# Gated delta layer's seam: panel splits ahead of the barrier, the first convolution first on VectorE, projections between the small products

## The chip, the cores and the metric

One core of one Trainium2 chip runs the kernel. The metric is the device time of one execution in microseconds (us).

## The reference, cut to what matters

The program computes two pairs of layers on 512 tokens of width 1024, all in float32: first a block with two attention mixers, each followed by a SwiGLU feed-forward layer, then a gated delta layer (GDN) and a gated linear attention layer (GLA), each with a layer norm behind it. The change lies at the start of the gated delta layer:

```
p    = x @ w_in                                   # 8 heads: q, k (128 wide), v (256), gate (256); and b, a
qkv  = silu(causal_conv(p[qkv], conv_w))          # 4 taps, per channel
q, k = l2norm(q), l2norm(k)
beta = sigmoid(b);  g = -exp(a_log) * softplus(a + dt_bias)
gc   = cumsum(g) in chunks                        # decays exp(gc_i - gc_j)
o    = gated_delta_rule(q, k, v, g, beta)         # a triangular solve per chunk, a state carried on
y    = (rmsnorm(o) * norm_w * silu(gate)) @ w_out
x    = layer_norm(DEEP_ALPHA * x + y)
```

## The kernel before, in words

**Precision.** Each float32 operand of a large matmul is split into an upper part (a cast, `high`, or a copy on ScalarE) and a lower part (the rest, `low`, on VectorE). `mm3` then issues three matmuls for one: upper by upper, upper by lower, lower by upper (lines 223 to 225 of the profile). Weights come in panels of 128 x 2048 (1 MB) in a ring of four slots; `landed`, `used` and `split` are semaphores of a slot: loaded, released by TensorE, and split into `hi_ring` and `lo_ring`. Line 195 is the load, 216 and 219 are `high` and `low`.

**Two blocks.** The program has two blocks with a barrier of all engines between them (line 4095 in the profile). The first ends with the second feed-forward layer and the "early" part of the gated delta layer. There, SP loads the three panels of head 0 (slots 1, 2 and 3), the constants and `ba_w`, the small weight for beta and alpha. VectorE splits slot 1's panel, then alternates: a residual addition `dve_ffn_add` (line 1782), and for the piece before it the lower part, for which ScalarE's `act_gdn_early` (line 2546) has made the upper part. TensorE's `pe_gdn_early` does 7 of 8 steps of the first projection, `project(0, 0)`. The second block begins with `pe_gdn`, `act_gdn`, `dve_gdn` and `sp_gdn`; GpSimd adds the eight pieces of x at its start (`pool_total`, lines 3325 and 3328).

**The seam behind the barrier.** The queues' orders are written out by hand. TensorE: the last step of `project(0, 0)` (3 matmuls), `project(0, 1)` (24 matmuls of 512 columns), `beta_alpha` (16; lines 2585, 2586), half of `project(0, 2)` (12), `turn_beta_alpha` (line 2593), `q_sums` (line 244), `key_products` (line 2645), `cumulate` (lines 2599, 2601), `pe_ln_mean` (line 3296), the other half of `project(0, 2)`, `project(0, 3)` (24), `row_decays` (line 2651), and then `chain(0, None, 1)`. Projections share two banks of PSUM, so `project(h, 2)` waits for the convolution of 0 and `project(h, 3)` for that of 1.

VectorE: the split of `ba_w`, of panels 2 and 3, the taps (line 3027), `convolve(0, 0)` and `convolve(0, 1)` (one operation on line 3036 and three on 3038 each), the beta/alpha arithmetic (lines 3236 to 3246), the norms of q and k (3069 to 3077), the accumulated decays (3251, 3252), `convolve(0, 2)`, `columns_of` (3044 to 3052), `log_decays` (3063, 3064), its chain. ScalarE: the copy of the beta/alpha rows (line 2987), Silu of the first two convolutions (`convolved`, line 2873), the square of q, Exp and Ln for the decay (2992 to 2995), Ln of the norms, Exp and Sigmoid for the columns (2998, 2999), Silu of the third, the mean's copy, `decays` (2901 to 2904). Changing the function often costs an `ACT_TABLE_LOAD`.

**The chain** of a head solves the triangular system by doubling, six levels; each level is a pair of small products on TensorE (line 2756 and 2774) with VectorE's mask or addition between (3167, 3173). Ahead of it stand the decays and the first mask (A and Qh, lines 3146, 3150), which line 2744's turn of 64-column blocks waits for. Between the small products TensorE has "fills": in head 0 these are `project_gate(0, t)` for t = 0 to 3 (24 matmuls of 256 columns each), then the projections of head 1:

```
            def first_fill(part):
                ...
                elif p is None:
                    project_gate(i, 0, part * DC // 2, (part + 1) * DC // 2)
```

`first_fill(0)` stands before the turn, `first_fill(1)` behind it, then level 1's first product, `fill(1)`, its step product (line 2774) and `fill(2)`. VectorE answers the turn (line 3159), then does `convolve(0, 3)`, the taps of head 1 and two pieces of centring, and after that level 1's first product (line 3167), which the step product waits for. Heads 1 to 6 run in a loop, the last by itself; the change touches none of them.

Of the kernel before, what the change touches and what calls it, by code (L numbers as in the profile page):

```python
# [104 lines left out]
def build_in(nc, io, ctx):  # L105
# [2437 lines left out]
    def act_gdn_early(act):  # L2543
        for c in range(DC):
            act.wait_ge(S("ffn_added"), after("ffn1", "added", c + 1))
            nc.scalar.copy(h_hi[:, c, :], xT[:, c, :]).then_inc(S("g_x_upper"), 1)

    def dve_gdn_early(dve):
        for c in range(DC + 1):
            if c < DC:  # L2550
                dve_ffn_add(dve, "ffn1", c)
            if c:
                dve.wait_ge(S("g_x_upper"), c)
                low(h_lo[:, c - 1, :], xT[:, c - 1, :], h_hi[:, c - 1, :]).then_inc(S("ffn_x_split"), 1)

# [24 lines left out]
    def pe_gdn(pe):  # L2580
        def beta_alpha():

            pe.wait_ge(S("g_ba_split"), 1)
            for k in range(DC):
                mm(ps[0:BA_ROWS, 0, :], ba_parts[:, k, :], h_hi[:, k, :], start=k == 0, stop=False)
                last = mm(ps[0:BA_ROWS, 0, :], ba_parts[:, k, :], h_lo[:, k, :], start=False, stop=k == DC - 1)
            last.then_inc(S("g_ba_rows"), 1)
# [110 lines left out]
        def chain(i, p, h):  # L2698

            def first_fill(part):  # L2700
                if h is None:
                    output_part(p, *((0, 5), (5, 8))[part])
                elif p is None:
                    project_gate(i, 0, part * DC // 2, (part + 1) * DC // 2)
                else:
                    output(p, part, part + 1)

            def fill(place):
                if h is None:
                    start = 8 + 4 * (place - 1) - max(0, place - 8)  # L2710
                    output_part(p, start, start + (4 if place < 8 else 3))
                elif place < 4:
                    if p is None:
                        project_gate(i, place)
                    else:
                        output(p, 2 * place, 2 * place + 2)
                else:
                    c, half = divmod(place - 4, 2)
                    project(h, c, half * DC // 2, (half + 1) * DC // 2, gated=p is None)
# [125 lines left out]
        project(0, 1, 0, DC, first=True)  # L2845
        beta_alpha()
        project(0, 2, 0, DC // 2, first=True)
        turn_beta_alpha()
        q_sums(0)
# [3 lines left out]
        project(0, 2, DC // 2, DC, first=True)  # L2853
# [16 lines left out]
    def act_gdn(act):  # L2870
# [20 lines left out]
        def squares(h):  # L2891
            act.wait_ge(S("g_silu"), h * 4 + 2)
# [92 lines left out]

        act.wait_ge(S("g_ba_rows"), 1)
        nc.scalar.copy(ba_rows, ps[0:BA_ROWS, 0, :]).then_inc(S("g_ba_saved"), 1)
        convolved(0, 0)
        convolved(0, 1)
# [5 lines left out]
        nc.scalar.activation(z_l[:, :, :], z_e[:, :, :], ACT.Ln, bias=1.0).then_inc(S("g_zl"), 1)  # L2995
        norms(0)
        act.wait_ge(S("g_cum_cols"), 1)
        nc.scalar.activation(col_all(LAST), ps[:, 7, 0:TT * GH].rearrange("p (t h) -> p t h", t=TT), ACT.Exp).then_inc(S("g_col_exp"), 1)
        nc.scalar.activation(col_all(BETA), ba[:, :, 0:GH], ACT.Sigmoid).then_inc(S("g_col_exp"), 1)
# [9 lines left out]
    def dve_gdn(dve, link):  # L3009
# [215 lines left out]
        w, hi, lo = ba_w[:, :, :], ba_parts[:, :, 0:2 * GH], ba_parts[:, :, 2 * GH:BA_ROWS]  # L3225
        link(high(hi, w))
        low(lo, w, hi)
        nc.vector.tensor_tensor(ba_pairs, ident[0:BA_ROWS, 0:2 * GH], ident[0:BA_ROWS, 2 * GH:BA_ROWS], ALU.add).then_inc(S("g_ba_split"), 1)
        split_panel(dve, link, 2, 0)
        link(nc.vector.memset(U[second, :, first], 0.0))  # L3230
        conv_taps(0)
        split_panel(dve, link, 3, 0)
        convolve(0, 0)
        convolve(0, 1)
# [11 lines left out]
        nc.vector.tensor_copy(col_all(G), z_e[:, :, :])  # L3246
        q_variances(0)
# [787 lines left out]
    with nc.Block() as block:  # L4035
# [21 lines left out]
        def _(dve):  # L4057
# [16 lines left out]
            dve_gdn_early(dve)  # L4074
# [213 lines left out]
```

## Time and profile before

| | us |
|---|---|
| median of 3 runs | 2162.68 (2158.27 to 2166.95) |
| profiled execution, its span | 2162.8 |
| TensorE busy | 2092.5 |
| VectorE busy | 1475.1 |
| ScalarE busy | 958.6 |
| mean granted TensorE clock | 0.983 |

The page gives the span of the profiled execution and no other time for it; it is within 0.2 us of the median of the runs. Times in the trace count from the span's start. The barrier opens at 1280.86, and the first block takes the 1280 us before it. Only the some 60 us behind the barrier are at issue; where TensorE stands still there, and at which clock it runs, is to be read in the trace.

### The profile page before, as it was taken

The numbers are of one execution on the slowest core, as the hardware profiler recorded it, in microseconds if no ns is written. First come the engines' busy times: TensorE is split into PE (matmuls) and PEld (weight loads), VectorE is DVE, ScalarE is ACT, GpSimd is POOL, SyncE is SP. The second block draws the span as 40 slices with busy tenths as digits, with TensorE's granted clock in tenths as the row PEclk, the third lists the DMA queues.
The fourth block names the chain that finished last, engine by engine and source line by source line (L and its number), as shares of the span: only waits on it lengthen the run. The fifth ranks groups of instructions, "written<-read, shape, count | busy, mean of one in ns | idle before, by whom it ended". The sixth has DMA issues, their size and how long they took to land. (4 is left out here: it accounts for less than half of the span.)

```text
span 2162.8 us, 37677 instructions
## 1 busy us (share of the span) xinstructions
PE 2092.5 (97%) x15185; PEld 1802.0 (83%) x15185; DVE 1475.1 (68%) x2901; ACT 958.6 (44%) x1853; POOL 80.8 (4%) x47
## 2 busy tenths in 40 slices
PE   8998999999999999999999989999999999899997
PEld 8996667899988977889998867878887888688886
DVE  5347884988854677598886465666666666576566
ACT  5336872555400367345550014434443444356554
POOL 1110000000000300000000020000000000020000
PEclk9999999999999999999999998999999999999998
DMA  5230001232332320123323221111111110112211
GB/s 181 97 117 21 2 2 59 88 117 98 108 117 85 108 74 21 59 70 103 112 90 135 89 77 59 59 60 58 58 58 58 58 58 34 55 46 98 79 40 40
DMA packets 30666, 159.37 MB, mean 74 GB/s; under 512 B 3392, under 2 KB 3904, under 8 KB 17856
## 3 DMA queue, kind: packets, MB, share of 16 engines
q1 hardware_dynamic: 30240, 157.24, 20.5%
q8 instruction: 98, 1.61, 0.3%
q14 instruction: 40, 0.33, 0.0%
q10 hardware_dynamic: 288, 0.20, 0.0%
HBM read 155.33 MB, written 2.10 MB: 73 GB/s over the span
## 5 line engine op out<-in xcount | busy, mean ns | idle before, releaser
L224 PE MATMUL ps<-late_parts,panel_upper 128*128 128x256 f32 (+1 forms) x1376 | 460.2, 334 | 0.0
L223 PE MATMUL ps<-late_parts,panel_upper 128*128 128x256 f32 (+1 forms) x1260 | 433.6, 344 | 2.6 <-issue 1.8
L225 PE MATMUL ps<-late_parts,panel_parts 128*128 128x256 f32 (+1 forms) x1260 | 425.6, 338 | 0.0
L219 DVE TENSOR_TENSOR panel_parts<-panel_sb,panel_upper 128x512 fp32r<-128x512 f32 (+1 forms) x334 | 329.1, 1011 | 12.8 <-ACT panel_upper L723 8.4
L223 PE MATMUL ps<-panel_upper,hT_parts 128*128 128x256 f32 (+2 forms) x964 | 297.5, 309 | 7.3 <-DVE h_lower L911 7.3
L225 PE MATMUL ps<-panel_upper,h_lower 128*128 128x256 f32 (+2 forms) x964 | 285.4, 296 | 0.0
L224 PE MATMUL ps<-panel_parts,hT_parts 128*128 128x256 f32 (+2 forms) x964 | 284.3, 295 | 0.0
L224 PEld LDWEIGHTS ps<-late_parts,panel_upper 128*128 128x128 f32 x1376 | 260.2, 189 | 26.0 <-issue 0.2
L223 PEld LDWEIGHTS ps<-late_parts,panel_upper 128*128 128x128 f32 x1260 | 238.2, 189 | 32.9 <-issue 2.4
L225 PEld LDWEIGHTS ps<-late_parts,panel_parts 128*128 128x128 f32 x1260 | 239.2, 190 | 28.7
L223 PE MATMUL ps<-hT_parts,panel_upper 128*128 128x512 f32 (+1 forms) x508 | 203.8, 401 | 10.0 <-DVE arena_sb L3038 5.8
L223 PEld LDWEIGHTS ps<-panel_upper,hT_parts 128*128 128x128 f32 x964 | 184.5, 191 | 12.1 <-issue 7.9
L225 PE MATMUL ps<-hT_parts,panel_parts 128*128 128x512 f32 (+1 forms) x508 | 194.3, 382 | 0.0
L225 PEld LDWEIGHTS ps<-panel_upper,h_lower 128*128 128x128 f32 x964 | 185.0, 192 | 3.1
L224 PEld LDWEIGHTS ps<-panel_parts,hT_parts 128*128 128x128 f32 x964 | 184.0, 191 | 3.5
L224 PE MATMUL ps<-h_lower,panel_upper 128*128 128x512 f32 x432 | 174.4, 404 | 0.0
L1525 ACT CAST panel_upper<-panel_sb 128x512 fp32r<-128x512 f32 x230 | 132.6, 621 | 12.5 <-DVE panel_sb L1640 11.4
L223 PEld LDWEIGHTS ps<-hT_parts,panel_upper 128*128 128x128 f32 x508 | 96.7, 190 | 35.1 <-DVE arena_sb L3038 6.3
L225 PEld LDWEIGHTS ps<-hT_parts,panel_parts 128*128 128x128 f32 x508 | 96.8, 191 | 20.6
L224 PEld LDWEIGHTS ps<-h_lower,panel_upper 128*128 128x128 f32 x432 | 82.6, 191 | 17.6 <-issue 0.8
L2926 ACT COPY arena_sb<-ps 128x256 f32<-128x256 f32 (+1 forms) x40 | 14.9, 372 | 173.9 <-PE ps L2761 138.5
L3038 DVE SCALAR_TENSOR_TENSOR arena_sb<-ps,arena_sb 128x511 f32<-128x511 f32 (+2 forms) x96 | 71.9, 748 | 3.4
(531 smaller groups left out, 3787.6 us busy)
## 6 DMA issues: line engine op xcount, KB each, us to landing
panel_sb<-ffn_gate_up_w SPq DMA_DIRECT2D x76, 512.0 KB, 4.4
panel_sb<-gdn_w SPq DMA_DIRECT2D x24, 1024.0 KB, 4.8
panel_sb<-ffn_down_w SPq DMA_DIRECT2D x22, 1024.0 KB, 4.8
panel_sb<-nsa_w SPq DMA_DIRECT2D x13, 1024.0 KB, 5.0
panel_sb<-gla_w SPq DMA_DIRECT2D x12, 1024.0 KB, 4.8
panel_sb<-gdn_out_w SPq DMA_DIRECT2D x8, 1024.0 KB, 4.8
panel_sb<-ffn_gate_up_w SPq DMA_DIRECT2D x6, 1024.0 KB, 4.8
panel_sb<-nsa_out_w SPq DMA_DIRECT2D x4, 1024.0 KB, 4.7
```

The source lines that it names most:

```text
L219: return engine.tensor_tensor(out, src, hi.bitcast(F32), ALU.subtract)
L223: mm(out, w_hi, x_hi, start=start, stop=False, skip_group_check=skip_group_check)
L224: mm(out, w_hi, x_lo, start=False, stop=False, skip_group_check=skip_group_check)
L225: return mm(out, w_lo, x_hi, start=False, stop=stop, skip_group_check=skip_group_check)
L1525: nc.scalar.copy(hi, plain).then_inc(S("ffn_high"), 1)
L2926: nc.scalar.copy(Xh[r, :, :], ps[r, 3, 0:TT * HALF].rearrange("p (t c) -> p t c", t=TT)).then_inc(S("g_x"), 1)
L3038: last = nc.vector.scalar_tensor_tensor(conv[n][:, back:T], src[:, 0:T - back], hconv[:, n, 3 - back:4 - back], conv[n][:, back:T], ALU.mu ...
```

## The change

Ahead of the barrier: ScalarE makes the upper part of panel 2 before, and of panel 3 after its eight casts of x; VectorE makes the lower part of panel 2 before the residual additions, and the split of `ba_w` (with `ba_pairs`) behind them. Behind the barrier: VectorE begins with the taps and the first convolution, then the lower part of panel 3; the second convolution moves behind the beta/alpha arithmetic. ScalarE does Silu of the first convolution before the copy of the beta/alpha rows, the square of q before the second Silu, and the Sigmoid directly behind the Ln. TensorE does `beta_alpha` before `project(0, 1)`, `turn_beta_alpha` in its middle, and all of `project(0, 2)` before `q_sums`. In head 0's chain, `first_fill(0)` is all of `project_gate(0, 0)` and `first_fill(1)` the first half of `project_gate(0, 1)`, with the other half left to `fill(1)`.

```diff
     def act_gdn_early(act):
+        def upper(slot):
+            act.wait_ge(landed[slot], (act_panels.done[slot] + 1) * 16)
+            nc.scalar.copy(hi_ring[slot][:, :, :], ring[slot][:, :, :]).then_inc(S("g_early_upper"), 1)
+
+        upper(2)
         for c in range(DC):
...
+        upper(3)
+
+    def dve_gdn_early(dve, link):
+        dve.wait_ge(S("g_early_upper"), 1)
+        low(lo_ring[2][:, :, :], ring[2][:, :, :], hi_ring[2][:, :, :]).then_inc(split[2], 1)
         for c in range(DC + 1):
...
+        dve.wait_ge(S("gdn_const_landed"), 32)
+        w, hi, lo = ba_w[:, :, :], ba_parts[:, :, 0:2 * GH], ba_parts[:, :, 2 * GH:BA_ROWS]
+        link(high(hi, w))
+        low(lo, w, hi)
+        link(nc.vector.tensor_tensor(ba_pairs, ident[0:BA_ROWS, 0:2 * GH], ident[0:BA_ROWS, 2 * GH:BA_ROWS], ALU.add))
...
         def beta_alpha():
-            pe.wait_ge(S("g_ba_split"), 1)
...
                 elif p is None:
-                    project_gate(i, 0, part * DC // 2, (part + 1) * DC // 2)
+                    project_gate(i, *((0, 0, DC), (1, 0, DC // 2))[part])
...
                     if p is None:
-                        project_gate(i, place)
+                        project_gate(i, place, DC // 2 if place == 1 else 0, DC)
...
         project(0, 0, DC - 1, DC, first=True)
-        project(0, 1, 0, DC, first=True)
         beta_alpha()
-        project(0, 2, 0, DC // 2, first=True)
+        project(0, 1, 0, DC // 2, first=True)
         turn_beta_alpha()
+        project(0, 1, DC // 2, DC, first=True)
+        project(0, 2, 0, DC, first=True)
         q_sums(0)
         key_products(0, 3)
         cumulate()
         pe_ln_mean(pe, 0, GDN_MEAN_BANK)
-        project(0, 2, DC // 2, DC, first=True)
         project(0, 3, 0, DC, first=True)
...
         def squares(h):
-            act.wait_ge(S("g_silu"), h * 4 + 2)
+            act.wait_ge(S("g_silu"), h * 4 + 1)
...
+        convolved(0, 0)
         act.wait_ge(S("g_ba_rows"), 1)
         nc.scalar.copy(ba_rows, ps[0:BA_ROWS, 0, :]).then_inc(S("g_ba_saved"), 1)
-        convolved(0, 0)
-        convolved(0, 1)
         squares(0)
...
         nc.scalar.activation(z_l[:, :, :], z_e[:, :, :], ACT.Ln, bias=1.0).then_inc(S("g_zl"), 1)
+        nc.scalar.activation(col_all(BETA), ba[:, :, 0:GH], ACT.Sigmoid).then_inc(S("g_col_exp"), 1)
+        convolved(0, 1)
         norms(0)
         act.wait_ge(S("g_cum_cols"), 1)
         nc.scalar.activation(col_all(LAST), ...
-        nc.scalar.activation(col_all(BETA), ba[:, :, 0:GH], ACT.Sigmoid).then_inc(S("g_col_exp"), 1)
         convolved(0, 2)
...
-        w, hi, lo = ba_w[:, :, :], ba_parts[:, :, 0:2 * GH], ba_parts[:, :, 2 * GH:BA_ROWS]
-        link(high(hi, w))
-        low(lo, w, hi)
-        nc.vector.tensor_tensor(ba_pairs, ident[0:BA_ROWS, 0:2 * GH], ident[0:BA_ROWS, 2 * GH:BA_ROWS], ALU.add).then_inc(S("g_ba_split"), 1)
-        split_panel(dve, link, 2, 0)
+        conv_taps(0)
+        convolve(0, 0)
+        low(lo_ring[3][:, :, :], ring[3][:, :, :], hi_ring[3][:, :, :]).then_inc(split[3], 1)
         link(nc.vector.memset(U[second, :, first], 0.0))
-        conv_taps(0)
-        split_panel(dve, link, 3, 0)
-        convolve(0, 0)
-        convolve(0, 1)
         dve.wait_ge(S("g_ba"), 1)
...
         nc.vector.tensor_copy(col_all(G), z_e[:, :, :])
+        convolve(0, 1)
         q_variances(0)
```

## Rows read from the trace of the kernel before

**Rows 1.** The page: engines' busy time, granted clock in 40 slices, gated delta panels' loads
```profile
PE 2092.5 (97%) x15185; PEld 1802.0 (83%) x15185; DVE 1475.1 (68%) x2901; ACT 958.6 (44%) x1853; POOL 80.8 (4%) x47
...
PEclk9999999999999999999999998999999999999998
...
panel_sb<-gdn_w SPq DMA_DIRECT2D x24, 1024.0 KB, 4.8
```

**Rows 2.** Waits from 1240 to 1400 us: us in total, times, longest
```profile
ACT hT_parts L2546 <- DVE xT_sb L1782: 118.4, 8, 113.0
...
PE ps L223 <- DVE arena_sb L3038: 5.8, 1, 5.8
...
PE ps L2744 <- DVE arena_sb L3150: 2.4, 1, 2.4
...
PE ps L223 <- PEq L4095: 1.7, 1, 1.7
```

**Rows 3.** Stretches: length; busy us (instructions) by engine; granted clock; DMA share, GB/s
```profile
1280.86:1287.29 6.43, 6.43 (x27) 5.07 (x28) 5.62 (x5) 0.00 (x0) 6.20 (x4) 1.00 0.01 4
...
1291.16:1296.96 5.80, 0.00 (x1) 0.00 (x1) 5.69 (x6) 0.60 (x2) 5.04 (x3) 0.85 0.09 38
1296.96:1302.25 5.29, 5.29 (x13) 3.80 (x13) 2.85 (x4) 2.86 (x4) 0.00 (x0) 0.52 0.00 0
1302.25:1305.29 3.04, 3.04 (x25) 2.82 (x24) 0.79 (x4) 1.29 (x4) 0.00 (x0) 1.00 0.00 0
1305.29:1306.65 1.36, 0.00 (x1) 0.01 (x1) 0.41 (x3) 0.84 (x2) 0.00 (x0) 0.56 0.00 0
1306.65:1310.08 3.43, 3.43 (x16) 3.43 (x17) 1.68 (x5) 1.49 (x2) 0.00 (x0) 0.50 0.00 0
1310.08:1322.23 12.15, 12.11 (x39) 8.70 (x40) 5.73 (x16) 5.44 (x7) 0.00 (x0) 0.77 0.00 0
1322.23:1328.45 6.22, 3.85 (x26) 3.15 (x27) 4.23 (x15) 1.73 (x4) 0.00 (x0) 1.00 0.48 169
1328.45:1335.81 7.36, 7.36 (x68) 6.81 (x69) 7.19 (x14) 5.88 (x11) 0.00 (x0) 0.77 0.01 3
```

**Rows 4.** TensorE's timeline from `row_decays`: start, us, engine, line, operation, tiles, shapes
```profile
1322.23 1.10 PE L2651 MATMUL ps<-arena_sb,ones_sb 128*128 128x512 f32 x2
1323.17 0.60 PE L2732 MATMUL ps<-ident_sb,arena_sb 128*128 128x128 f32 x4
```

**Rows 5.** VectorE's timeline, before and behind the barrier (in brackets: idle before it)
```profile
1255.14 2.29 DVE L219 TENSOR_TENSOR panel_parts<-panel_sb,panel_upper 128x2048 fp32r<-128x2048 f32 x1
1264.48 0.69 DVE L1782 TENSOR_TENSOR xT_sb<-xT_sb,ps 128x512 f32<-128x512 f32 x1 [7.05 <-PE ps L225]
...
1281.60 0.61 DVE L216 CAST late_parts<-arena_sb 128x128 fp32r<-128x128 f32 x1 [5.25 <-PEq L4095]
...
1284.91 3.27 DVE L219 TENSOR_TENSOR panel_parts<-panel_sb,panel_upper 128x2048 fp32r<-128x2048 f32 x1
...
1293.82 0.74 DVE L3036 TENSOR_SCALAR arena_sb<-ps,arena_sb 128x512 f32<-128x512 f32 x1
...
1303.35 0.22 DVE L3236 COPY arena_sb<-ps 128x64 f32<-128x64 f32 x1 [3.43 <-PE ps L2593]
...
1319.67 0.17 DVE L3044 COPY arena_sb<-arena_sb 128x20 f32<-128x20 f32 x1
...
1334.23 0.42 DVE L3167 TENSOR_TENSOR arena_sb<-ps,arena_sb 128x256 f32<-128x256 f32 x1
```

**Rows 6.** ScalarE's timeline: the last cast before the barrier, a table load behind it
```profile
1275.01 0.62 ACT L2546 CAST hT_parts<-xT_sb 128x512 fp32r<-128x512 f32 x1 [0.78 <-DVE xT_sb L1782]
...
1304.62 1.28 ACT L2995 ACT_TABLE_LOAD   x1
1305.91 0.23 ACT L2995 ACTIVATE arena_sb<-arena_sb 128x32 f32<-128x32 f32 x1
```

**Rows 7.** SP's timeline: the load of head 0's second panel (slot 2)
```profile
1251.88 0.33 SPq L195 DMA_DIRECT2D panel_sb<-gdn_w  x1
```

More of the change, by code:

```diff
@@ L2546, in act_gdn_early @@
             nc.scalar.copy(h_hi[:, c, :], xT[:, c, :]).then_inc(S("g_x_upper"), 1)
-    def dve_gdn_early(dve):
+        upper(3)
+    def dve_gdn_early(dve, link):
+        dve.wait_ge(S("g_early_upper"), 1)
+        low(lo_ring[2][:, :, :], ring[2][:, :, :], hi_ring[2][:, :, :]).then_inc(split[2], 1)
         for c in range(DC + 1):
@@ L4073, in _ @@
             dve_ffn(dve, link, "ffn1", ahead=True)
-            dve_gdn_early(dve)
+            dve_gdn_early(dve, link)
         @block.gpsimd
```

## The prediction

> **What bounds the kernel now.** I read the page first. TensorE is busy for 97% of the span and its granted clock is full nearly everywhere [rows 1], so time is won only where TensorE stands still or runs at the lower of its two levels (1.2 instead of 2.4 GHz). The page's forty slices are too coarse for that, so I next read TensorE's waits around the barrier [rows 2]: one of 5.8 us for the first convolution of VectorE, 2.4 us for VectorE's level mask in the first chain, and 1.7 us at the barrier. Then I cut the seam into stretches, with the clock of each [rows 3]. From the barrier (1280.86) to `row_decays` (1322.23) pass 41.37 us. Up to 1291.16 the clock is full and nothing waits. Then TensorE waits 5.80 us and runs at 0.50 to 0.56 until 1310, but for the three small products at 1.00; over the last 12.15 us the mean is 0.77. So the wait is paid for twice: 5.80 us of standing still, then half speed.
>
> Why that wait is there: VectorE's row from 1281 on [rows 5] has the beta/alpha split, both panel splits (one lower part takes 3.27 us) and the taps ahead of the first convolution, which starts at 1293.82. Its input was ready near 1281.8, when `project(0, 0)` ended.
>
> **Before the barrier.** Six steps move there: upper and lower part of slot 2, the upper part of slot 3 (both upper parts now ScalarE's), and three small ones for beta/alpha. The lower part of slot 3 stays behind, after the first convolution. ScalarE has waited 113.0 us for the first residual addition [rows 2], VectorE has been idle for 7.05 us before 1264.48 [rows 5]. Slot 2's load is issued at 1251.88 [rows 7] and such loads land in 4.8 us [rows 1], so at 1256.7. ScalarE's upper part (not in this stretch; a 128x512 cast took 0.62 us [rows 6], this is four times as long, so 1.3 to 2.5 us; I take 1.9) ends at 1258.6, VectorE's lower part (2.29 us without GpSimd beside it [rows 5]) at 1260.9: 3.6 us to spare before the first residual addition. Slot 3's upper part follows the last of eight casts on ScalarE, which ends at 1275.6 [rows 6], so it runs to 1277.5; VectorE's three small beta/alpha operations follow the one lower part (0.7 us) that this cast releases, and end near 1277.5 too. TensorE reaches the barrier only at 1279.2 (1.7 us before 1280.86 [rows 2, 3]), and the barrier opens for all at once. So these steps cost nothing; 1.6 us of cover is what ScalarE has. SP issues the same loads in the same order; slot 1's next load is issued some 5 us later (its panel is released after the second half of `project(0, 1)`), 25 us and more ahead of its use.
>
> **TensorE from the barrier to `row_decays`.** No matmul is added or taken. A 512-column matmul at full clock costs 6.43/27 = 0.238 us [rows 3]. I take the stretches of before and price each at full clock and without its wait [rows 3]:
> - the wait for the first convolution: 5.80 us gone;
> - 12 matmuls of `project(0, 2)`: 5.29 instead of 2.86, saves 2.43;
> - the wait ahead of `cumulate`: 1.36 gone;
> - `cumulate` at 0.50: 3.43 becomes 1.71, saves 1.72;
> - the mean and 36 matmuls: 12.15 becomes 0.94 (the like product of `row_decays`, from its start to the next [rows 4]) + 36 x 0.238 = 9.51, saves 2.64.
>
> Sum 13.95 us: `row_decays` at 1308.3.
>
> That holds if VectorE and ScalarE are in time. Followed through: VectorE begins at 1281.6 [rows 5]; a convolution is four operations of 0.74 us [rows 5], 3.0 us, so the first is done at about 1285.3, and with Silu and the copy of the rows (0.6 us each) `ba_rows` stand at 1286.6. TensorE comes to `turn_beta_alpha` at 1288.2, after 3 + 16 + 12 matmuls. VectorE meanwhile lowers slot 3 (3.27 us beside GpSimd) and sets U, until 1289.0; the turned beta/alpha come at 1289.3 (a small product group takes 1.0). From there to g ready took 1303.35 to 1306.65, 3.3 us [rows 3, 5]: 1292.6, then the second convolution to 1295.9 and its Silu to 1296.6. TensorE needs that after `project(0, 2)` and the sums, at 1298.7. Its sums, key products, `cumulate` and mean run to 1302.5. VectorE takes `cumulate`'s result at 1301.6, convolves the third until 1305.1, and needs 2.5 us for the columns (1319.67 to `row_decays` at 1322.23 [rows 4, 5]): 1307.6, against 1308.3 on TensorE. VectorE is the next one late, by a margin of only 0.7 us here and 2.1 us at the key products.
>
> ScalarE gets two table loads more (Sigmoid and Silu now stand between two Ln). A load takes 1.28 us and the next activation starts 1.29 us after it [rows 6]; both fall into its waits. The Trainium skill (ScalarE: Activation LUTs, What ACT_TABLE_LOAD costs) gives about 2.66 us for a switch, a drain on top of the load; by that figure the sum would be some 2 us less. No row here shows such a drain.
>
> **The first chain.** Before, `row_decays` to the 64-column turn took 6.22 us, the last 2.4 idle, and from there to the first step product 7.36 us [rows 2, 3]. VectorE sets both ends: decays and mask for the first; for the second its answer to the first level, at 1334.23 + 0.42 = 1334.65 [rows 5], 6.2 us after the turn. The change moves 12 gate matmuls (256 columns each, half of 0.238, so 1.4 us) from behind the turn to before it, and 12 others from `fill(1)` into their place. The first idle shrinks to 1.0, and TensorE now waits about 2 us for VectorE where it used to arrive 1.2 us late: step product 12.4 after `row_decays` instead of 13.58, a gain of 1.1. The clock there was 0.77 over 7.36 us, a loss of about 1.7 hidden in part; with a new idle of 2 us the lower clock comes somewhat later, when it is not hidden. I bound that from -0.5 to +2.0 us and take 1.1, the gain given back. The chains behind are the same, and TensorE-bound.
>
> **Sum.** 13.95 + 1.1 - 1.1 = 13.9 us off the span of 2162.8 us (the page gives no other time for that execution, and the median of the three runs is 2162.68): 2148.9 us. A difference of 0.5%, 10.8 us, is about what a measurement of this kernel can tell from none; the runs of before lie 4 us to each side of their median.
>
> **Rivals.**
> 1. **The clock falls in the small products.** 25 records, nearly all of small products, at 1.00 were followed at once by 0.56 [rows 3]. The change puts sums, key products, `cumulate` and mean in one row of 4.7 us. If it falls there, `cumulate` (1.7), mean (0.9) and 12 matmuls behind (2.4) are at half speed again, 5.0 us lost: 2153.9. Against it: the stretch from 1322.23, small products with 12 gate matmuls, stayed at 1.00. Chance 0.18. The Trainium skill (TensorE: Matmul & The Clock Gate, Part 1) has the throttled clock as the default that activity releases; the rows at 0.50 behind idle and thin work agree.
> 2. **VectorE or ScalarE becomes the bound.** The margins above are 0.3 us for slot 3's lower part before beta/alpha and 0.7 at the columns, and beside GpSimd VectorE's operations are longer by up to 1 us (3.27 against 2.29 [rows 5]). Some such delays, 2 us in all with a lower clock behind, leave TensorE waiting at the key products and at `row_decays`: 4 to 8 us given back, 2155. Chance 0.12.
> 3. **The order on the chip doesn't become what the diff says**, a remaining wait (g_conv for `project(0, 2)`) being met late all the same: 2162.8. For it only that the first convolution still waits for `project(0, 0)`; against it, that this is ready 12 us before its use. Chance 0.04.
> 4. **Slower: the hoisted split blocks the residual additions.** VectorE now waits for slot 2's upper part ahead of all eight additions, and TensorE's early projection and ScalarE's casts stand behind them. Each us by which the panel lands after 1260.3 (3.6 later than reckoned) is a us lost; it outweighs 13.9 us from a landing at 1274 on, and at 1285, if the load queued that long, gives 2174. Landings of 4.8 us [rows 1] speak against it. Chance 0.03.
> 5. **A table switch holds ScalarE for twice its load.** Then the seven loads up to the decays cost 9 us more; those ahead of the second Silu (three, 3.9 us) and between the diagonal and the saved mean (two, 2.6 us) are on TensorE's path, once past the margins of 2.1 and 1.9 us: about 2 us lost, 2151. Against it: the activation 1.29 us behind a load [rows 6]. Chance 0.02; this is what the skill's figure above would do.
>
> **How the numbers follow.** My forecast gets the rest, 0.61, and by itself spans 2145 (clock never falls in the chain, 1.1 + 0.5 more, with scatter of the median) to 2151.5. Taking in rival 1 and most of rival 2, down to 2156, leaves out no more than 2 in 10. Faster by over 0.5% means below 2151.9: nearly all of the forecast (0.60), a third of rival 1 and a little of rival 2: 0.70. Rival 4 gives slower, 0.03; the rest, 0.27, is within 0.5%.
>
> **What would show it.** In the trace of after: VectorE's first convolution within 2 us of the barrier; no wait of TensorE of over 0.5 us between barrier and `row_decays`; that stretch 27 to 28 us long with a clock near 1.00 (0.9 and 31 to 33 us under rival 1); a TensorE wait for VectorE of about 2 us at the first step product; first residual addition still at 1264.5 and the barrier still 1280.9 (rival 4 if not). It is wrong if the 5.80 us wait appears under another name, at the key products or ahead of `row_decays`, or if the chains behind take longer than before.

## The result, and the profile after

| | before | after |
|---|---|---|
| median of the runs, us | 2160.47 (4 runs, 2157.96 to 2166.95) | 2143.9 (4 runs, 2143.52 to 2147.01) |
| profiled execution: span; mean granted clock | 2162.8; 0.983 | 2141.7; 0.992 |
| from the barrier to `row_decays` | 41.37 | 27.02 |
| from `row_decays` to the first step product | 13.58 | 12.44 |

The ratio is 0.9916 (0.99 to 0.9931), which of 2160.47 us is 18.1 us; the medians lie 16.6 us apart. The forecast was 13.9 us and 2148.9 us. The result lies under the forecast, and 1.1 us under the 2145 us that the prediction gives as the low end of its own span. First the profile after. The page, its busy times and its slices with the clock:

```profile
PE 2077.3 (97%) x15185; PEld 1789.2 (84%) x15185; DVE 1472.5 (69%) x2899; ACT 964.9 (45%) x1857; POOL 76.5 (4%) x47
...
PEclk9999999999999999999999999999999999999998
```

Against [rows 1] the same 15185 matmuls are busy for 15.2 us less: work that ran at half clock no longer does. The forty slices hardly show it. TensorE's waits from 1240 to 1400 us (total, times, longest):

```profile
PE ps L2786 <- issue: 1.8, 1, 1.8
PE ps L223 <- PEq L4102: 1.7, 1, 1.7
PE ps L2756 <- DVE arena_sb L3162: 0.9, 1, 0.9
```

The 5.8 us of [rows 2] are gone, and no new name stands in their place before `row_decays`. The 2.4 us of the level mask became 0.9, and a new wait of 1.8 us stands at the first step product, as forecast. The stretches of after, with the columns of [rows 3]: barrier to `row_decays`; in it the unbroken row of small products (sums, key products, `cumulate`); `row_decays` to the turn; the turn to the first step product; and what follows that:

```profile
1279.09:1306.11 27.02, 26.98 (x134) 20.81 (x135) 20.26 (x38) 14.88 (x20) 10.97 (x7) 1.00 0.12 40
1295.90:1300.13 4.23, 4.19 (x36) 3.87 (x34) 2.31 (x7) 2.29 (x4) 0.00 (x0) 1.00 0.00 0
1306.11:1312.25 6.14, 5.22 (x39) 4.51 (x38) 4.24 (x15) 1.73 (x4) 0.00 (x0) 1.00 0.50 173
1312.25:1318.55 6.30, 4.53 (x56) 4.08 (x57) 6.13 (x13) 5.39 (x11) 0.00 (x0) 1.00 0.00 1
1318.55:1322.10 3.55, 3.55 (x41) 3.48 (x42) 3.55 (x6) 0.48 (x1) 0.00 (x0) 1.00 0.00 0
```

TensorE is busy for 26.98 of 27.02 us, at full clock. The two changed stretches together take 39.46 instead of 54.95 us: **15.5 us saved**. The two spans differ by 21.1 us, so 5.6 us more came from elsewhere; the experiments say whether they belong to the change.

VectorE's timeline, the pre-barrier lower part and the first residual addition; the first convolution behind the barrier; then the turned beta/alpha with its arithmetic (idle time before an instruction in brackets):

```profile
1257.41 2.29 DVE L219 TENSOR_TENSOR panel_parts<-panel_sb,panel_upper 128x2048 fp32r<-128x2048 f32 x1 [1.77 <-ACT panel_upper L2546]
1262.68 0.69 DVE L1782 TENSOR_TENSOR xT_sb<-xT_sb,ps 128x512 f32<-128x512 f32 x1 [2.98 <-PE ps L225]
...
1280.43 0.75 DVE L3048 TENSOR_SCALAR arena_sb<-ps,arena_sb 128x512 f32<-128x512 f32 x1
...
1287.60 0.23 DVE L3242 COPY arena_sb<-ps 128x64 f32<-128x64 f32 x1 [0.59 <-PE ps L2605]
1287.86 1.31 DVE L3243 TENSOR_TENSOR arena_sb<-arena_sb,vec_sb 128x32 f32<-128x32 f32 x1
1289.21 0.18 DVE L3244 TENSOR_SCALAR arena_sb<-arena_sb 128x32 f32<-128x32 f32 x1
1289.42 1.16 DVE L3245 TENSOR_TENSOR arena_sb<-arena_sb 128x32 f32<-128x32 f32 x1
```

The first addition still waits for TensorE, for 2.98 us, so the hoisted lower part delays nothing (rival 4 is out). The convolution starts 1.3 us behind the barrier, where in [rows 5] it started 13.0 us behind it. ScalarE's timeline, the hoisted upper part of slot 3 and the second Silu, and TensorE's key products:

```profile
1273.73 1.90 ACT L2546 CAST panel_upper<-panel_sb 128x2048 fp32r<-128x2048 f32 x1
...
1296.20 0.63 ACT L2885 ACTIVATE arena_sb<-arena_sb 128x512 f32<-128x512 f32 x1 [0.84 <-DVE arena_sb L3050]
```

```profile
1296.88 1.16 PE L2657 MATMUL ps<-arena_sb 128*128 128x128 f32 x8
```

ScalarE's 1.90 us are what the prediction took, and end at 1275.6, ahead of TensorE's last matmul before the barrier. The Silu ends at 1296.83, and the key products that need it start at 1296.88: of the forecast margin of 2.1 us nothing is left. They even wait a little: they start 0.98 us behind the sums (1295.90), where in delay2 below, with the Silu done well before, it is 0.80 us. These 0.2 us are too short for the list of waits.

### The profile page after: what moved, and what is told of

Read it like the earlier page. It is cut to its first block and busy times, and to the rows that moved or that the text cites. A ratio compares the mean times of both kernels' runs of the same rounds, so it can differ in the third digit from the quotient of the medians.

```text
span 2141.7 us, 37681 instructions
## 1 busy us (share of the span) xinstructions
PE 2077.3 (97%) x15185; PEld 1789.2 (84%) x15185; DVE 1472.5 (69%) x2899; ACT 964.9 (45%) x1857; POOL 76.5 (4%) x47
```

## The experiments

The theory: VectorE's queue behind the barrier makes the 5.8 us wait, and that wait and thin small products lower the clock; take both away and the stretch costs what its matmuls cost at full clock. Rivals: TensorE's order alone does it; the hoist alone does it; the gain depends on where the clock falls by chance. The kernels ran in three batches on three chips, each with its own runs of before beside it: the first down to fills_old (before's median 2163.94), the second from pe_only to delay4 (2164.5), the third from "changed, third" on (2163.67). All times in us; "stretch" is barrier to `row_decays`, "chain" is `row_decays` to the first step product.

| kernel | median (n) | ratio to before | stretch | chain |
|---|---|---|---|---|
| changed, again | 2148.27 (5) | 0.9925 (0.9912 to 0.9939) | 27.01 | 12.45 |
| hoist_only | 2153.76 (5) | 0.9954 (0.9941 to 0.9968) | 31.87 | 13.60 |
| pe_old | 2162.02 (11) | 0.999 (0.9981 to 0.9999) | 38.56 | 13.60 |
| fills_old | 2148.2 (5) | 0.9926 (0.9912 to 0.9939) | 28.59 | 13.44 |
| pe_only | 2154.75 (5) | 0.9959 (0.9945 to 0.9973) | 35.58 | 12.45 |
| centre_later | 2148.64 (4) | 0.9931 (0.9915 to 0.9948) | 28.60 | 11.24 |
| delay2 | 2148.47 (4) | 0.9933 (0.9917 to 0.995) | 28.21 | 12.44 |
| delay4 | 2151.35 (4) | 0.9945 (0.9929 to 0.9962) | 29.61 | 12.45 |
| changed, third | 2148.95 (5) | 0.9931 (0.9916 to 0.9947) | 27.01 | 12.44 |
| spread | 2147.7 (5) | 0.9924 (0.9909 to 0.994) | 27.04 | 11.24 |
| cum3 | 2154.49 (1) | | 32.07 | 12.44 |
| fills_old_b | 2148.45 (1) | | 27.02 | 13.48 |

### The changed kernel again, twice

No edit. The first expectation:

> The changed kernel once more, beside the kernel before. Theory: the change is worth what the two traces show between the barrier and the first step product of head 0's chain, 15.5 us (41.37 to 27.0, and 13.58 to 12.4); the other 5.6 us between the two profiled executions lie in stretches that the change does not touch and differ by the granted clock alone, so over five rounds the difference should come to 15 to 17 us. Rival: the change also does something for the stages behind it, and the difference stays at 18 us or more.

And the second, in the third batch:

> The changed kernel a third time, as the measure for spread beside it. Theory: 15 to 17 us faster than before; barrier to row_decays 27.0 us, or 28.6 if the clock falls in the small products; step product 12.4 us after row_decays.

Measured: medians 15.7 us (2163.94 less 2148.27) and 14.7 us (2163.67 less 2148.95) under before's, the second just short of the 15 to 17 us expected. TensorE's timeline of the first, with the barrier's wait, `row_decays` and the first step product:

```profile
1281.82 0.47 PE L223 MATMUL ps<-hT_parts,panel_upper 128*128 128x512 f32 x1 [1.70 <-PEq L4102]
1308.83 1.02 PE L2663 MATMUL ps<-arena_sb,ones_sb 128*128 128x512 f32 x2
1321.28 0.68 PE L2786 MATMUL ps<-arena_sb 64*64 64x64 f32 x16 [1.78 <-issue]
```

And of the second:

```profile
1283.75 0.47 PE L223 MATMUL ps<-hT_parts,panel_upper 128*128 128x512 f32 x1 [1.70 <-PEq L4102]
1310.76 1.02 PE L2663 MATMUL ps<-arena_sb,ones_sb 128*128 128x512 f32 x2
1323.20 0.68 PE L2786 MATMUL ps<-arena_sb 64*64 64x64 f32 x16 [1.77 <-issue]
```

The changed stretches repeat to 0.01 us in three executions. What stands around them doesn't: the same kernel comes to its barrier at 1279.09, 1281.82 and 1283.75, where before came at 1280.86. The first residual addition of after stands 1.8 us earlier than before's [rows 5] already, and the program up to a few us ahead of it is the same in both. That part of the 5.6 us, then, is scatter.

A further 0.9 us is spread over the rest. The other large part, 2.9 us, lies in the seam with the gated linear attention, over matmuls 13100 to 13500 of the program, from 1852.34 to 1930.39 in before: 78.05 us, and in after 75.18, again 75.13, third 77.02. (The expectations quote 48.1 and 50.9 us for this seam; these figures leave out some 27 us of it, and differ by nearly as much as 75.1 and 78.0, which are the whole.) The layer norm inside it can be read as stretches. Before:

```profile
1885.93:1925.68 39.75, 35.51 (x183) 28.77 (x183) 28.77 (x38) 19.68 (x32) 13.50 (x9) 0.83 0.21 76
```

and the same work in after:

```profile
1867.25:1905.51 38.26, 34.02 (x183) 27.22 (x183) 29.17 (x38) 19.68 (x32) 13.15 (x9) 0.87 0.22 79
```

and in the third execution:

```profile
1873.15:1912.07 38.92, 34.70 (x184) 27.79 (x184) 28.51 (x38) 19.68 (x32) 13.18 (x9) 0.87 0.21 77
```

The same matmuls and about the same idle time, 4.2 us in each; the busy time differs, with the clock. Over all executions the whole seam goes from 75.1 to 78.2 us, for kernels with and without any part of the change (hoist_only 77.97, delay2 75.15, delay4 77.94, spread 78.17). It is where the clock falls in that execution, and no effect of the change was found there. Executions of the changed kernel over the three batches: 14, from 2143.5 to 2151.8 us. The first four sat at the low end of them.

### Only the steps ahead of the barrier (before plus the hoist)

Before, with `act_gdn_early` and `dve_gdn_early` as in the change, and:

```diff
-            pe.wait_ge(S("g_ba_split"), 1)
...
-        link(high(hi, w))
-        low(lo, w, hi)
-        nc.vector.tensor_tensor(ba_pairs, ...).then_inc(S("g_ba_split"), 1)
-        split_panel(dve, link, 2, 0)
         link(nc.vector.memset(U[second, :, first], 0.0))
         conv_taps(0)
-        split_panel(dve, link, 3, 0)
+        low(lo_ring[3][:, :, :], ring[3][:, :, :], hi_ring[3][:, :, :]).then_inc(split[3], 1)
```

> The kernel before with only the steps moved ahead of the barrier (upper and lower part of slot 2, upper part of slot 3, the beta/alpha split); behind it VectorE sets U, copies the taps, lowers slot 3 and convolves 0 and 1 as before, TensorE and ScalarE keep their old orders and fills. Theory (VectorE's queue ahead of the first convolution made the wait): first convolution starts 5 us behind the barrier and ends at 8.3, before TensorE needs it at 10.3, so the 5.8 us wait is gone; 1.4 us ahead of cumulate stay and the clock falls there. Barrier to row_decays 29 us at full clock, up to 32 with it low: 9 to 12 us faster than before. Rival (the orders behind the barrier matter most): less than 6 us.

Measured: 10.2 us faster than before. The stretch, and in it what follows `cumulate`:

```profile
1279.34:1311.21 31.87, 30.46 (x134) 22.92 (x134) 18.18 (x38) 12.31 (x18) 11.18 (x7) 0.89 0.10 34
1299.23:1311.21 11.98, 11.93 (x40) 8.56 (x40) 5.73 (x16) 6.16 (x8) 0.00 (x0) 0.78 0.00 0
```

Its waits, without the barrier's:

```profile
PE ps L2756 <- DVE arena_sb L3162: 2.4, 1, 2.4
...
PE ps L2611 <- DVE arena_sb L3251: 1.4, 1, 1.4
```

With VectorE's queue emptied, TensorE's old order loses its 5.8 us wait. What stays is the 1.4 us ahead of `cumulate`, and the low clock behind it. The cause that the prediction named is right, and the steps ahead of the barrier bring about two thirds by themselves.

### Only TensorE's order and fills (before plus these)

```diff
         project(0, 0, DC - 1, DC, first=True)
-        project(0, 1, 0, DC, first=True)
         beta_alpha()
-        project(0, 2, 0, DC // 2, first=True)
+        project(0, 1, 0, DC // 2, first=True)
         turn_beta_alpha()
+        project(0, 1, DC // 2, DC, first=True)
+        project(0, 2, 0, DC, first=True)
         q_sums(0)
...
-        project(0, 2, DC // 2, DC, first=True)
...
```

with the two `project_gate` lines of the change besides.

> The kernel before with TensorE's new order and new fills alone; all splits stay behind the barrier and VectorE and ScalarE keep their old orders. Theory: TensorE waits about 2 us for the beta/alpha split right behind the barrier and 2.7 us for the first convolution, which still ends 16 us behind the barrier; the second is done at 19, so nothing waits at the key products. Barrier to row_decays 32 us at full clock, 34 if it falls: 8 to 10 us faster than before with the chain. Rival (the hoist is needed for any gain): within 4 us of before.

Measured: 9.75 us faster than before (2164.5 beside it). The stretch, and what follows the first step product:

```profile
1281.75:1317.33 35.58, 33.15 (x133) 23.62 (x134) 26.21 (x44) 12.52 (x18) 15.05 (x7) 0.81 0.09 30
...
1329.78:1334.86 5.08, 5.08 (x41) 5.01 (x42) 4.84 (x6) 0.48 (x1) 0.00 (x0) 0.66 0.01 3
```

Its wait that hoist_only has not:

```profile
PE ps L2585 <- DVE arena_sb L3228: 1.9, 1, 1.9
```

TensorE now meets the unsplit beta/alpha weights (1.9 us) and has work enough to cover the late convolution but for 0.2 us (2.7 were expected), but its clock is 0.81 over the stretch, which takes 35.58 us where 34 were expected at most. 10.2 and 9.75 us add up to more than the 15.7 of the whole: both halves remove the same 5.8 us wait. The second row shows the loss that the prediction reckoned with and after escaped: behind the 1.8 us wait at the step product the clock fell, and 3.55 us of work took 5.08.

### VectorE's and ScalarE's new order under TensorE's old one (pe_old)

After, with the order of before in TensorE's program, and the two `project_gate` lines of before:

```diff
         project(0, 0, DC - 1, DC, first=True)
+        project(0, 1, 0, DC, first=True)
         beta_alpha()
-        project(0, 1, 0, DC // 2, first=True)
+        project(0, 2, 0, DC // 2, first=True)
         turn_beta_alpha()
-        project(0, 1, DC // 2, DC, first=True)
-        project(0, 2, 0, DC, first=True)
         q_sums(0)
...
+        project(0, 2, DC // 2, DC, first=True)
```

> The changed kernel with TensorE's old order and old fills; the hoist and the new orders of VectorE and ScalarE stay. Theory: beta/alpha are turned at 14.2 us behind the barrier, VectorE then does their arithmetic (3.3) and only then the second convolution (3.0), whose Silu the key products wait for: a wait of 6 us at the key products and a low clock behind it. Barrier to row_decays 34 us at full clock, up to 39 with it low: 3 to 8 us faster than before, and slower than hoist_only. Rival (TensorE's order is of no weight once the splits are away): within 2 us of the changed kernel.

The stretch, in it the part from the wait on, and the wait:

```profile
1281.63:1320.19 38.56, 32.20 (x134) 24.63 (x134) 18.15 (x38) 14.99 (x20) 10.95 (x7) 0.82 0.07 28
1302.99:1320.19 17.20, 17.15 (x63) 13.76 (x63) 7.28 (x19) 6.64 (x8) 0.00 (x0) 0.69 0.00 0
```

```profile
PE ps L2657 <- ACT arena_sb L2885: 6.3, 1, 6.3
```

Nearly all is lost: 1.9 us faster than before, where the expectation had 3 to 8. The stretch itself is at the long end of what was expected (39). The second convolution now stands behind the beta/alpha arithmetic, and the old order turns beta/alpha late, so a wait of 6.3 us for the second Silu takes the place of the 5.8 us. Compared with hoist_only, the new VectorE and ScalarE orders without the TensorE order cost 8.3 us. The prediction had said how it would be wrong, with this wait at the key products; it is what half of the reordering gives.

### The old fills in the changed kernel (fills_old, twice)

```diff
-                    project_gate(i, *((0, 0, DC), (1, 0, DC // 2))[part])
+                    project_gate(i, 0, part * DC // 2, (part + 1) * DC // 2)
...
-                        project_gate(i, place, DC // 2 if place == 1 else 0, DC)
+                        project_gate(i, place)
```

> The changed kernel with the old fills in head 0's chain. Barrier to row_decays as changed, 27 us. The turn is answered by VectorE 6.2 us after row_decays and level 1 another 6.2 us later, whatever the fills are. Theory A (the fills' place earns the 1.1 us of the forecast): the step product comes 13.6 us after row_decays, 1.1 us slower than changed. Theory B (it was the low clock that made TensorE late there): if the clock stays high the step product comes at 12.4 to 12.5 with the old fills too, if it falls at 13.6.

The second time, in one execution:

> fills_old once more, for the chain: step product 13.4 to 13.6 us after row_decays if the 2.4 us wait ahead of the turn makes the clock fall again (as in all four traces with the old fills so far), 12.4 if it doesn't.

The first execution, from the mean to `row_decays`, and then the chain:

```profile
1301.76:1309.89 8.13, 8.13 (x29) 5.97 (x28) 5.76 (x17) 5.39 (x7) 0.00 (x0) 0.79 0.00 0
1309.89:1323.33 13.44, 11.06 (x95) 9.91 (x93) 11.19 (x28) 7.62 (x15) 0.00 (x0) 0.87 0.24 80
```

The second execution, the chain:

```profile
1308.25:1321.73 13.48, 11.12 (x96) 9.88 (x94) 11.40 (x28) 7.61 (x15) 0.00 (x0) 0.87 0.23 80
```

The chain shows what the fills bring. All five executions with the old ones took 13.44 to 13.60, all seven with the new fills and the same VectorE order 12.44 or 12.45. With the old fills TensorE waits 2.4 us ahead of the turn and the clock falls behind it; with the new ones it waits 0.9 and then 1.8 us, and the clock stays. So 1.1 us, repeatable in the trace and too small for the medians (2148.2 against 2148.27 beside it). Whether the old fills would cost anything with a clock that stays was not seen: it fell in all five. The first of the three rows, which begins with the mean, is rival 1 in one execution: at the end of the small products the clock fell (0.79), and the stretch took 28.59 instead of 27.02, 1.6 us.

### VectorE's centrings behind the level mask (centre_later)

```diff
-            adds(0)
+            else:
+                adds(0)
             for l in range(1, LEVELS):
...
+                if p is None and l == 1:
+                    adds(0)
                 adds(2 * l - 1)
```

> The changed kernel, with VectorE's first two centrings of x behind its answer to level 1 instead of ahead of it. Theory: the 1.8 us wait at the first step product shrinks to 0.5 us, so the step product comes 11.2 us after row_decays and the program reaches every later stage 1.2 us earlier. Whether the whole gains 1.2 us depends on the layer norm's seam near 1870: there the traces with one low stretch (changed, fills_old) took 48.1 us over the same matmuls and those with three (before, hoist_only, pe_old) 50.9. Theory P (what decides is at which moment the program comes there): another moment, so up to 2.8 us worse there, and the total from 1.2 faster to 1.6 slower than changed. Rival (the change itself makes that seam faster): 48.1 us there, 1.2 us faster in all.

The chain shrank by 1.2 us to 11.24, its wait from 1.8 to 0.6 us, as expected. The stretch of this execution was 28.60: the clock fell in its small products too. The median (2148.64) can't be told from that of the changed kernel in the other batches.

### Six and twelve extra matmuls ahead of `project(0, 2)` (delay2, delay4)

```diff
+        pe.wait_ge(S("g_conv"), 1)
+        split_ready(pe, 2, 0)
+        for again in range(2):
+            mm3(ps[:, PROJ_BANK, :], (hi_ring[2][:, 0, :], ...), (h_hi[:, 0, :], ...), True, True)
         project(0, 2, 0, DC, first=True)
```

delay4 has `range(4)`. The projection that follows overwrites the bank, so the added products have no effect on the result.

> The changed kernel with 6 idle-filling matmuls (the first of project(0, 2) done twice more) ahead of project(0, 2): 1.4 us more of dense TensorE work, nothing else. Theory P: the stages behind come 1.4 us later, and the layer norm's seam near 1870 takes 48.1 or up to 50.9 us by the moment at which it is reached; total 1.4 to 4.2 us slower than changed. Rival: 48.1 us there, 1.4 us slower.

> The changed kernel with 12 such matmuls, 2.8 us. Theory P: by this shift the program reaches the layer norm's seam at the moment, relative to the clock's steps, at which hoist_only did (three low stretches): 50.9 us there, so 5 to 6 us slower than changed in all. Rival: 48.1 us there, 2.8 us slower.

The stretch took 28.21 and 29.61: 1.20 and 2.60 us more for 1.40 and 2.80 us of matmuls (in delay2 ten of them in a row start 0.233 us apart, 1296.00 to 1298.33). So TensorE sets this stretch nearly throughout. The 0.2 us that are missing in both are the short wait for the second Silu in the changed kernel. In delay2 that Silu is done at 1298.57, the sums start at 1299.03, and the key products follow 0.80 us behind them instead of 0.98:

```profile
1299.83 1.14 PE L2657 MATMUL ps<-arena_sb 128*128 128x128 f32 x8
```

The seam of the layer norm took 75.15 us with delay2 and 77.94 with delay4, which is what Theory P said of them, but the totals did not follow. No run of the changed kernel stood beside these two. Delay4's median lies 3.1 and 2.4 us above those of again and third, not 5 to 6, and delay2's (2148.47) lies between theirs, where at least 1.4 us more was expected. Two executions don't show that the moment of arrival decides. Behind delay2's step product the clock fell once more as in pe_only:

```profile
1321.48:1326.57 5.09, 5.09 (x40) 5.02 (x41) 4.84 (x6) 0.48 (x1) 0.00 (x0) 0.66 0.00 0
```

That is 2 of 9 executions with the new fills, each at a cost of 1.5 us. Both are among the 7 that wait 1.8 us ahead of the step product; centre_later and spread wait 0.6 us there.

### Small products without any wait (cum3)

```diff
-            for t in range(TT):
-                mm(ps[:, 5, t * GH:(t + 1) * GH], triu, z_e[:, t, :], start=True, stop=True)
+            for again in range(3):
+                for t in range(TT):
+                    mm(ps[:, 5, t * GH:(t + 1) * GH], triu, z_e[:, t, :], start=True, stop=True)
```

The first half of `cumulate` is computed three times, with the same values.

> The changed kernel with the first half of cumulate issued three times (16 records of 128x8 more, the same values). If small products without any wait let the clock fall, it falls in this row of 5.8 us and project(0, 3) begins at half speed: barrier to row_decays 27.0 + 1.6 + 1.6 to 3 us, 30 to 32. Rival (only a standing TensorE does that): clock 1.00 and 28.6 us.

One execution, the small products in three pieces and the whole stretch:

```profile
1297.99:1299.97 1.98, 1.94 (x17) 1.85 (x16) 0.43 (x2) 1.66 (x2) 0.00 (x0) 1.00 0.00 0
1299.97:1303.30 3.33, 3.33 (x27) 3.33 (x25) 1.55 (x3) 1.71 (x3) 0.00 (x0) 0.77 0.00 0
1303.30:1305.00 1.70, 1.70 (x9) 1.70 (x10) 0.00 (x0) 0.03 (x1) 0.00 (x0) 0.50 0.00 0
...
1281.18:1313.25 32.07, 32.03 (x150) 25.08 (x151) 20.26 (x38) 14.88 (x20) 10.98 (x7) 0.89 0.09 33
```

TensorE is busy all the time (32.03 of 32.07), and yet its clock goes from 1.00 to 0.50 in the row of small products: in this execution no wait was needed, thin matmuls alone let it fall. Rival 1's mechanism exists. In the changed order, whose small products are 4.2 us long, it struck in 2 of 8 executions, for 1.6 us. The prediction had priced it at 5.0.

### The small products laid apart (spread)

```diff
-        project(0, 2, 0, DC, first=True)
+        project(0, 2, 0, DC // 2, first=True)
         q_sums(0)
+        project(0, 2, DC // 2, DC, first=True)
         key_products(0, 3)
         cumulate()
+        project(0, 3, 0, DC // 2, first=True)
         pe_ln_mean(pe, 0, GDN_MEAN_BANK)
-        project(0, 3, 0, DC, first=True)
+        project(0, 3, DC // 2, DC, first=True)
```

with the edit of centre_later besides.

> centre_later with q_sums in the middle of project(0, 2) and the layer norm's mean in the middle of project(0, 3), so that the longest row of small products is 3 us instead of 4.2. Theory (the row of small products is what lets the clock fall in some executions, at 1.6 us each): barrier to row_decays 27.0 us and a clock of 1.00 there, step product 11.3 us after row_decays; 0 to 2 us faster than the changed kernel beside it, which five rounds may not tell apart, since the layer norm's seam still takes 48 to 51 us by the moment of arrival. Rival (3 us of small products are enough): 28.6 us as in fills_old.

The stretch and the chain:

```profile
1281.32:1308.36 27.04, 27.04 (x133) 20.65 (x134) 20.16 (x38) 14.88 (x20) 10.98 (x7) 1.00 0.11 40
1308.36:1319.60 11.24, 9.75 (x95) 8.59 (x94) 9.16 (x25) 5.93 (x15) 0.00 (x0) 1.00 0.28 95
```

Both are what was aimed at, 38.28 us together against 39.45 for the changed kernel beside it. The medians are 2147.7 and 2148.95, 1.25 us apart. That is the right size, but the intervals of the two ratios overlap nearly whole, and one execution with an undisturbed clock proves nothing where the changed order too kept it in 6 of 8. It is at best 1.2 us better; that it beats the changed kernel wasn't shown.

## Why the prediction was right, and where it was not

**Before the barrier: right.** ScalarE's upper part took the 1.90 us assumed; VectorE's lower part left 2.98 us of cover ahead of the first addition, where 3.6 was reckoned; slot 3's upper part ended at 1275.6. Nothing was paid.

**TensorE from the barrier to `row_decays`: right.** The five terms gave 13.95 us, measured were 14.35 in each of three executions (41.37 less 27.02 or 27.01). Some 0.2 of the 0.4 us are the price of a matmul: 0.238 us has the slower first one behind the barrier in it, the rest start 0.233 us apart, over 48 matmuls. hoist_only shows whose wait it was, pe_only and pe_old that each half of the reordering brings less without the other.

**VectorE and ScalarE follow-through: right in the outcome, and one duration wrong.** `g ready` was put 3.3 us behind the turned beta/alpha, from the rows of before. In after the like way took 5.47 us (1287.60 to the second convolution at 1293.07). Two 128x32 operations took 1.31 and 1.16 us, where those of before's row took 0.19; the prediction had moved them to a place where GpSimd works beside them and had not charged for that. The delay of 2.1 us used up the margin of 2.1 us at the key products, and TensorE waited 0.2 us there. Slot 3's lower part was charged so (3.27), and came at 3.18.

**Table loads: right.** Two more of 1.28 us, each hidden. In pe_old, whose ScalarE has the new order, one reads as follows:

```profile
1298.62 1.28 ACT L3007 ACT_TABLE_LOAD   x1
1299.92 0.26 ACT L3007 ACTIVATE arena_sb<-arena_sb 128x32 f32<-128x32 f32 x1
```

The activation follows 1.30 us behind the load's start. The Trainium skill (ScalarE: Activation LUTs, What ACT_TABLE_LOAD costs) gives some 2.66 us with a drain; neither this row nor any other load of the stretch shows a drain, and rival 5 is out.

**The first chain: the +1.1 right, the -1.1 wrong.** The chain shrank from 13.58 to 12.44, forecast 12.4. The clock given back behind the new wait was charged in full, while it happens in 2 of the 7 executions with that wait, at 1.5 us, 0.4 us on average. In the profiled execution it cost nothing: the 3.55 us behind the step product ran at 1.00. The Trainium skill (TensorE: Matmul & The Clock Gate, Part 1) has the chip set the clock by how busy TensorE has been of late, and the moment of the switch vary from run to run; two falls in seven behind the like wait agree. The Trainium skill has idle time there as what lowers it, and cum3 shows a fall without any. That the clock stood at 0.77 behind the turn before was no ground for charging it behind a shorter wait at another place.

**The sum.** 13.9 us were forecast; 15.5 us stand in the changed stretches, and the three batches give 16.6, 15.7 and 14.7. The 1.6 us between 13.9 and 15.5 are the 1.1 of above, 0.4 in the five terms, and rounding.

**The range: this is the step that failed.** The mechanism held; what was mis-sized in the sum is the clock given back (1.1 us, in the profiled execution 0), and in the low end, which allowed for that, the scatter of a median. The low end of 2145 us is the forecast of 2148.9 less the 1.6 us by which the chain could do better (1.1 + 0.5), which leaves 2.3 us for scatter. The same kernel scatters by 8 us from one execution to another, and its medians of four or five runs lay at 2143.9, 2148.27 and 2148.95, those of before (4 to 15 runs) at 2160.47 to 2164.5. With 3 us for each of the two medians, 4.2 us together as the root of their squares, the low end comes to 2148.9 - 1.6 - 4.2 = 2143.1: an estimate, from the scatter that the later runs show. The base was loose too. An execution of this kernel lasts 1.8 us longer than its span (2144.4 and 2146.19 for again, 2160.1 and 2161.84 for pe_old), so before's profiled execution took some 2164.6 us, an estimate (none of the four runs beside after has this time), and the span of 2162.8 us, from which the forecast was counted, lay near the median of its runs by chance. That the medians of again and third lie within 1 us of the forecast is in part luck: before's, beside them, were 1.0 to 1.3 us higher than the 2162.68 of the forecast, and the gains were 15.7 and 14.7 instead of 13.9.

**The rivals.** Rival 1 is real and was priced three times too high, since the fall came late in the row of small products and the matmuls of 512 columns behind it brought the clock back: 1.6 us in 2 of 8. Rival 2 came to 0.2 us of waiting at the key products, not to the 4 to 8 it was priced at; the clock stayed at 1.00. Rival 3: each part does on the chip what the diff says. Rivals 4 and 5 are out. Slower was nowhere near.

## What to carry to other kernels

A wait of TensorE can be paid twice, as idle time and as half clock behind it: here that of 5.8 us was, those of 2.4 us in the chain were in all five executions, those of 1.8 us in 2 of 7. Cost both, and cost a move on one engine's queue only together with the orders of the others, since VectorE's new order without TensorE's put a wait of 6.3 us where one of 5.8 had been. Price a moved instruction by what works beside it in its new place, tiny ones too. And where the clock's phase differs from execution to execution, compare the stretch that was changed (here the same to 0.01 us), not the spans (here 5 us apart), and make a range for a median as wide as that scatter.

## What was not expected of the hardware

**Tiny operations beside GpSimd.** In after two 128x32 additions or products of VectorE between buffers took 1.31 and 1.16 us, while GpSimd worked on its six adds. The one of them beside the first (1287.86 to 1289.17):

```profile
1287.83 1.30 POOL L3335 TENSOR_TENSOR arena_sb<-arena_sb,xT_sb 128x512 f32<-128x512 f32 x1
```

Between the two the one with a single input took 0.18, though an add had begun 0.01 us ahead of it. In pe_old the same instructions come behind GpSimd's work, and take 0.19 us:

```profile
1296.07 0.19 DVE L3243 TENSOR_TENSOR arena_sb<-arena_sb,vec_sb 128x32 f32<-128x32 f32 x1
...
1296.51 0.19 DVE L3245 TENSOR_TENSOR arena_sb<-arena_sb 128x32 f32<-128x32 f32 x1
```

Each of the two began 0.03 and 0.22 us behind the start of an add and ended with it. So the 1 us added to each of them is the rest of an add already running, which takes 1.3 us. In hoist_only one sees both sides. The copy of the taps, with a single input, began behind an add and took 1.19 us, against 0.20 in after. The lower part began just ahead of one and took its 2.29 us, and the add took 3.42:

```profile
1280.70 1.29 POOL L3335 TENSOR_TENSOR arena_sb<-arena_sb,xT_sb 128x512 f32<-128x512 f32 x1
1280.83 1.19 DVE L3039 COPY arena_sb<-vec_sb 128x16 f32<-128x16 f32 x1
1282.05 2.29 DVE L219 TENSOR_TENSOR panel_parts<-panel_sb,panel_upper 128x2048 fp32r<-128x2048 f32 x1
1282.06 3.42 POOL L3335 TENSOR_TENSOR arena_sb<-arena_sb,xT_sb 128x512 f32<-128x512 f32 x1
```

So the price hangs on the moment, and GpSimd pays it as well. The convolution's first operation, which reads `ps`, took 0.75 us beside the adds and 0.74 elsewhere. The Trainium skill (SBUF — State Buffer, Terms) says that VectorE and GpSimd arbitrate for a pair of ports that one of them holds for a whole instruction, the other blocking meanwhile. The rows above agree. The Trainium skill (GPSIMD Engine Reference, Key points) names VectorE's instructions with two SBUF inputs as concerned, and those in a mode that uses two ports. The two of after agree; the copy has one input, and in which mode it ran no run shows. The way from the turned beta/alpha to the second convolution shows the price, 5.47 us in after against 3.37 in pe_old (1295.81 to 1299.18).

**Small matmuls lowered the clock without any idle time** (cum3, one execution), and **a wait of 1.8 us sometimes does and sometimes doesn't**: identical stretches were followed by 3.55 or 5.08 us.
